# A two-layer hybrid decoder step: router products with the router's weights stationary, in three column groups of TensorE

## The reference, cut to what matters

```python
x = layer_norm(ALPHA * x + h, prm['ln_mix_g'][layer], prm['ln_mix_b'][layer])
f = moe_ffn(x, prm['w_router'], prm['b_router'], ...)

def moe_ffn(x, w_router, b_router, w_gate, w_up, w_down):
    xt = x.reshape(Bn * T, D)
    probs = jax.nn.softmax((xt @ w_router).astype(jnp.float32) + b_router, axis=-1)
    ...
```

## Time and profile before

| | us |
|---|---|
| runs (3) | 1962.90 to 1966.55, median 1966.42 |
| the profiled execution | 1965.85 |
| its span | 1963.7 |
| `mix_out`, first PE product to last logits | 964.8 to 1129.3 |
| `combine_pool_mix`, first POOL fill to last logits | 1430.5 to 1573.7 |

### The profile page before, as it was taken

One profiled execution on the slowest core, in us unless ns is written; L12 is line 12 of the kernel. 1 busy time (PEld: TensorE's weight loads), 2 busy tenths in 40 slices (PEclk: granted clock), 3 DMA queues, 4 the chain that ended last, 5 costly groups with the idle time before them and its releaser, 6 DMA issues. The chain is left out here.

```text
span 1963.7 us, 29748 instructions
## 1 busy us (share of the span) xinstructions
PE 1602.3 (82%) x11876; PEld 1020.5 (52%) x11877; DVE 709.9 (36%) x1129; ACT 347.3 (18%) x753; POOL 230.4 (12%) x275
## 2 busy tenths in 40 slices
PE   6999996765522999985399949999959949999978
PEld 5666564544212888873145434444439834444433
DVE  1000000744965555546533341111159641111117
ACT  1000001541311322322000001111112201111111
POOL 3000000003002222303000001001040001100121
PEclk7999997885555999997699959999959959999989
DMA  7224201100011000000411267877750268887634
GB/s 230 99 93 121 107 1 33 46 23 5 0 27 23 4 4 4 4 6 5 118 44 33 94 232 272 294 278 275 243 193 1 88 211 282 288 289 240 212 141 168
DMA packets 134252, 237.09 MB, mean 121 GB/s; under 512 B 20434, under 2 KB 94147, under 8 KB 133866
## 3 DMA queue, kind: packets, MB, share of 16 engines
q1 hardware_dynamic: 110642, 150.94, 23.6%
q0 software_dynamic: 16880, 60.46, 8.4%
q10 hardware_dynamic: 6624, 24.12, 3.0%
HBM read 178.82 MB, written 58.21 MB: 121 GB/s over the span
## 5 line engine op out<-in xcount | busy, mean ns | idle before, releaser
L1985 PE MATMUL ex_pb<-ew_w_gate_up,ex_xT 128*128 x736 | 330.1, 602 | 5.9 <-DVE ex_xT L2025 2.3
L222 PE MATMUL pj_pb<-pj_xT,pj_w 128*128 128x344 f32 (+3 forms) x960 | 282.1, 457 | 0.4 <-ACT pj_xT L232 0.4
L222 PEld LDWEIGHTS pj_pb<-pj_xT,pj_w 128*128 128x128 f32 (+1 forms) x960 | 180.8, 188 | 101.2 <-issue 1.7
L1985 PEld LDWEIGHTS ex_pb<-ew_w_gate_up,ex_xT 128*128 128x128 f32 x736 | 137.9, 192 | 165.3 <-issue 164.4
L1968 PE MATMUL ex_pb<-ew_w_down,ex_hiddenT 128*128 x368 | 165.7, 593 | 3.4 <-ACT ex_hiddenT L2050 3.4
L2174 DVE TENSOR_TENSOR ex_hidden<-ex_hidden,ex_pb 128x256 f32<-128x256 f32 x46 | 19.4, 421 | 324.6 <-ACT ex_hidden L2045 324.6
L1968 PEld LDWEIGHTS ex_pb<-ew_w_down,ex_hiddenT 128*128 128x128 f32 x368 | 66.3, 190 | 69.9 <-issue 69.9
L1932 POOL COPY ex_tokens_now<-ex_token_of_slot 128x1 uint32 (+1 forms) x48 | 9.5, 199 | 745.5 <-PE ex_pb L1957 399.7
L1741 PE MATMUL mo_pb<-mo_w,projected 128*128 128x512 f32 (+1 forms) x144 | 65.8, 611 | 21.3 <-DMA mo_w<-in_w_out 21.3
L2169 DVE COPY ex_y_rows<-ex_pb 128x512 f32<-128x512 f32 x46 | 31.8, 692 | 134.5 <-PE ex_pb L1968 134.5
L238 DVE COPY projected<-pj_pb 128x344 f32<-128x344 f32 (+3 forms) x21 | 10.9, 519 | 187.9 <-PE pj_pb L222 187.9
(11 more groups left out here) (422 smaller groups left out, 2429.5 us busy)
## 6 DMA issues: line engine op xcount, KB each, us to landing
ew_w_gate_up<-in_w_ex_gate SPq DMA_DIRECT2D x32, 1024.0 KB
ew_w_gate_up<-in_w_ex_up SPq DMA_DIRECT2D x32, 1024.0 KB
ew_w_down<-in_w_ex_down SPq DMA_DIRECT2D x32, 1024.0 KB
scratch_slots_out<-ex_y_rows ACTq DMA_DIRECT2D x46, 512.0 KB
scratch_slots_out<-pj_zero POOLq DMA_DIRECT2D x4, 4096.0 KB
scratch_x_stored<-x_rows SPq DMA_DIRECT2D x16, 512.0 KB
pj_w<-in_w_in SPq DMA_DIRECT2D x3, 2048.0 KB, 18.6
pj_xt<-in_x_prompt SPq DMA_DIRECT2D x8, 512.0 KB
```

What stands on the lines that cost most here:

```text
L222: last = nc.tensor.matmul(pb[0:mrows, 4 + at % 4, 0:tn], w[:, s % NW, k, c0:c0 + mrows], xT[:, k, t0:t0 + tn], start=(k == 0), stop=(k == ...
L1985: last = mm(pb[:, 2 + u, :], xT[:, u, k, :], w[:, k, :], start=(k == 0), stop=(k == KD - 1))
```

## The change

The router's product is turned round. The weights become the stationary side: a k-slice of `wr`, now 32 columns wide (the 16 columns twice), is loaded into column group g = k % 3 of TensorE, and xT streams past it with up to 128 token columns. The three groups write partitions 0 to 31, 32 to 63 and 64 to 95 of bank 6, each the sum of its own k-steps, with tokens along the free side. ScalarE copies these 96 x 128 partial sums to SBUF (`copy_parts`), and one more product (`router_sum`) with the parts as the stationary side and a 96 x 16 matrix `sel` of zeros and ones adds the three groups and turns the result, into bank 7. `take_logits` reads bank 7.

So that this fits in, router_sum(j) stands at the head of the TensorE iteration behind router(j), ahead of the next transposes; it waits for ev >= j (bank 7 emptied of tile j-1) and for copy_parts(j). VectorE takes the logits one iteration later than before, in both stages. copy_parts(j) stands behind norm_root in ScalarE's order, in the pooling stage ahead of first_gate. GpSimd makes `sel` with two small additions at the start of each stage (`group_sums`), in the pooling stage ahead of the gathers, and `w_router` is loaded twice.

```diff
+RG, RW = 3, 32
+def router_columns(pe, bank, wr, xT, n):
+    for k in range(KD):
+        g = k % RG
+        last = pe.matmul(bank[RW * g:RW * g + RW, 0:n], wr[:, k, :], xT[:, k, 0:n], start=(k < RG), stop=(k + RG >= KD))
+    return last
+def group_sums(pool, eng, sel, ident, sem):
+    eng.tensor_tensor(sel[:, :], ident[0:RG * RW, 0:E], ident[0:RG * RW, RW:RW + E], ALU.add).then_inc(sem, 1)
+    pool.wait_ge(sem, 1)
+    eng.tensor_tensor(sel[:, :], sel[:, :], ident[0:RG * RW, 2 * RW:2 * RW + E], ALU.add).then_inc(sem, 1)
@@ combine_pool_mix, GpSimd @@
             nc.gpsimd.tensor_scalar(alpha_i[:, :], const["ident"][:, :], ALPHA, None, ALU.mult).then_inc(q["alpha"], 1)
+            group_sums(pool, nc.gpsimd, sel, const["ident"], q["sel"])
             for j in range(TILES):
                 gather(j)
@@ combine_pool_mix, TensorE @@
             for s in steps:
+                if live(s - 4):
+                    router_sum(s - 4)
                 if live(s - 3):
                     transposes(s - 3)
@@ combine_pool_mix, ScalarE @@
                     norm_root(nc, act, qa, s + 1, rows(ORDER[s + 1]), sta, eps)
+                if live(s - 3):
+                    copy_parts(s - 3)
                 if live(s + 2):
                     first_gate(s + 2)
@@ combine_pool_mix, VectorE @@
-                if live(s - 4):
-                    take_logits(s - 4)
+                if live(s - 5):
+                    take_logits(s - 5)
@@ mix_out, TensorE @@
+            def router_sum(i):
+                n = rows(i)
+                if i == 0:
+                    pe.wait_ge(q["sel"], 2)
+                else:
                     pe.wait_ge(q["ev"], i)
+                pe.wait_ge(q["rpc"], i + 1)
+                nc.tensor.matmul(pb[0:n, 7, 0:E], part[:, 0:n], sel[:, :], start=True, stop=True).then_inc(q["rl"], 1)
-            for i in range(TILES + LAG):
-                if i >= LAG:
+            for i in range(TILES + LAG + 1):
+                if i > LAG:
+                    router_sum(i - LAG - 1)
+                if LAG <= i < TILES + LAG:
                     transpose_x(i - LAG)
                 if i < TILES:
                     products(i)
-                if i >= LAG:
+                if LAG <= i < TILES + LAG:
                     router(i - LAG)
@@ mix_out, ScalarE @@
+            def copy_parts(i):
+                n = rows(i)
+                act.wait_ge(q["rp"], i + 1)
+                if i:
+                    act.wait_ge(q["rl"], i)
+                nc.scalar.copy(part[:, 0:n], pb[0:RG * RW, 6, 0:n]).then_inc(q["rpc"], 1)
             for i in range(TILES + LAG):
                 if i >= LAG:
                     copy_x(i - LAG)
                 if i < TILES:
                     norm_root(nc, act, q, i, rows(i), st, eps)
+                if i >= LAG:
+                    copy_parts(i - LAG)
@@ mix_out, VectorE @@
             for i in range(TILES):
-                if i > LAG:
-                    take_logits(i - LAG - 1)
+                if i > LAG + 1:
+                    take_logits(i - LAG - 2)
...
-            for i in range(TILES - LAG - 1, TILES):
+            for i in range(TILES - LAG - 2, TILES):
                 take_logits(i)
```

More of the change, by code:

```diff
@@ L1445, in combine_pool_mix @@
         alpha_i = m.sb("alpha_ident", [P, P])
+        part = m.sb("logit_parts", [RG * RW, P])
+        sel = m.sb("group_sums", [RG * RW, E])
         pb = m.psum("pb", [P, 8, 512])
@@ L1449, in combine_pool_mix @@
         qb = {k: m.sem(f"b_{k}") for k in LN}
-        q = {k: m.sem(k) for k in "eps alpha first both wscaled band feats tr cp rl ev zero keep".split()}
+        q = {k: m.sem(k) for k in "eps alpha sel first both wscaled band feats tr cp rp rpc rl ev zero keep".split()}
         s_r = [m.sem(f"rows{i}") for i in range(TILES)]
         block = m.block()
-        steps = range(-1, TILES + 4)
+        steps = range(-1, TILES + 5)
         def x_(j):
@@ L1539, in router, with router_sum @@
             def router(j):
-                n = rows(ORDER[j])
                 pe.wait_ge(q["cp"], j + 1)
                 if j:
+                    pe.wait_ge(q["rpc"], j)
+                router_columns(nc.tensor, pb[:, 6, :], pm.wr, xT, rows(ORDER[j])).then_inc(q["rp"], 1)
+            def router_sum(j):
+                n = rows(ORDER[j])
+                if j == 0:
+                    pe.wait_ge(q["sel"], 2)
+                else:
                     pe.wait_ge(q["ev"], j)
-                for k in range(KD):
-                    last = mm(pb[0:n, 6, 0:E], xT[:, k, 0:n], pm.wr[:, k, :], start=(k == 0), stop=(k == KD - 1))
-                last.then_inc(q["rl"], 1)
+                pe.wait_ge(q["rpc"], j + 1)
+                mm(pb[0:n, 7, 0:E], part[:, 0:n], sel[:, :], start=True, stop=True).then_inc(q["rl"], 1)
             for s in steps:
+                if live(s - 4):
+                    router_sum(s - 4)
                 if live(s - 3):
@@ L1583, in copy_feats, with copy_parts @@
                     .then_inc(q["feats"], 1)
+            def copy_parts(j):
+                n = rows(ORDER[j])
+                act.wait_ge(q["rp"], j + 1)
+                if j:
+                    act.wait_ge(q["rl"], j)
+                nc.scalar.copy(part[:, 0:n], pb[0:RG * RW, 6, 0:n]).then_inc(q["rpc"], 1)
             first_gate(0)
@@ L1686, in mix_out @@
         w = m.sb("w", [P, KD, D])
-        wr = m.sb("w_router", [P, KD, E])
+        wr = m.sb("w_router", [P, KD, RW])
+        part = m.sb("logit_parts", [RG * RW, P])
+        sel = m.sb("group_sums", [RG * RW, E])
         g = m.sb("ln_g", [P, D])
@@ L1694, in mix_out @@
         pb = m.psum("pb", [P, 8, 512])
-        q = {k: m.sem(k) for k in "in w w_rwkv0 w_rwkv1 mm res st var root rs g x tr cp rl ev eps zero".split()}
+        q = {k: m.sem(k) for k in "in w w_rwkv0 w_rwkv1 mm res st var root rs g x tr cp sel rp rpc rl ev eps zero".split()}
         s_x = [m.sem(f"x{i}") for i in range(2)]
@@ L1727, in _ @@
             pool.dma_start(b[:, :], io["ln_mix_b"][0:1, :].to_broadcast([P, D])).then_inc(q["in"], 16)
-            pool.dma_start(wr[:, :, :], io["w_router"].rearrange("(k p) e -> p k e", p=P)).then_inc(q["in"], 16)
+            for e0 in range(0, RW, E):
+                pool.dma_start(wr[:, :, e0:e0 + E], io["w_router"].rearrange("(k p) e -> p k e", p=P)).then_inc(q["in"], 16)
+            group_sums(pool, nc.gpsimd, sel, const["ident"], q["sel"])
             nc.gpsimd.memset(lg[:, NT, :], 0.0).then_inc(q["zero"], 1)
```

28 lines of the change are left out of this document (16 added, 12 removed).

## The result

The change makes the kernel slower. Its median is 2008.24 us (4 runs, 2003.16 to 2010.13) beside 1966.28 us for the kernel before in the same session: a ratio of 1.021, 95% interval 1.0193 to 1.0228. The profiled execution took 2010.13 us with a span of 2007.9, which is 44.3 us more than the profiled execution of before; 44.1 of them lie in `mix_out`.

What follows compares the result with a forecast made beforehand. TensorE bounds `mix_out` (busy 16.35 of 16.35 us); in pooling VectorE is almost level. `mix_out` +40.5, second w_router load +0.3, pooling -3.75: +37 on 1965.85, median 2003; own range 1996 to 2010, with two rivals 1988 to 2014.

Steps and rivals of the forecast that it cites:

- Part 1, the products: Router product in both stages: 0.81 us (0.66 plus 0.15) instead of 1.71, then copy 0.27 and sum about 0.25.
- columns don't overlap: Rival: column groups run one after another, a router product takes 1.9 us instead of 0.8; +10 us, 2013; chance 0.08.
- Part 2, the waits: In `mix_out` router_sum waits for copy_parts in iteration 3 (2.2 us), for take_logits in iterations 4 to 8 (4.5 each).
- P: End of tile i's projection on TensorE in a `mix_out` iteration; transposes were to move from P + 1.55 to P + 6.1.
- Part 3, the clock: Half clock behind the `mix_out` waits: 2.3 us in five iterations (11.5), 1.0 in iteration 3; the profile row gave 2.5.
- clock holds: Rival: the clock stays full through the `mix_out` waits; 12.5 us and 1.5 of the end fall away, 1989; chance 0.11.
- Part 4, the end of `mix_out`: Last residual to last logits in `mix_out` grows from 11.3 to 14.6 us: +3.3 (bounds 1.5 and 5).
- Part 5, the pooling stage: Pooling stage: three steady steps -0.9 us, end -3.7, start +0.85 from additions ahead of the gathers; sum -3.75.
- faster: the saving counts: Rival: router_sum's waits don't count, each of 18 products gives 0.65 us; -12 us, 1954; chance 0.03.
- the waits to be half as long: Rival: `mix_out` waits are shorter, say only ScalarE's 2.2 us eight times, half clock after some; 1985; chance 0.06.

## Why the prediction was right

Forecast +37 us on the profiled execution and a median of 2003; measured +44.3 and 2008.2. Sign, mechanism and stage were right, and the time was inside the range. Point by point:

- **Part 1, the products.** 0.78 us each from first start to the start of what follows (1048.07 to 1048.85 in the kernel with the sum behind the projection; predicted 0.66 + 0.15 = 0.81), or 0.85 to the last end; the copy of the parts 0.24 to 0.26 (0.27). The rival "columns don't overlap" is excluded by these rows and by the kernel with one group (1.93). The rule that the prediction weighed, the Trainium skill's "TensorE: Matmul & The Clock Gate", Part 3, by which matmuls start and end in strict program order, would have given nine slots of 0.11 here, 0.98 us. The trace does not agree: in that product the passes start in six bunches (four of three and two of two) 0.11 to 0.13 us apart, with no more than 0.013 us between the starts of one bunch. Two passes of one group start 0.11 us apart (the kernel with one group), so the starts of a bunch belong to different groups, and a pass starts before the second pass of the product ahead of it.
- **Part 2, the waits.** As predicted, once ended by ScalarE (2.66 us) and then six times by VectorE's logits (4.9 to 5.0, the last one in the stage's end), and the transposes at P + 6.1, the predicted value. Wait per iteration 4.4 to 4.6 (predicted 4.5), and 2.1 (2.2) in iteration 3.
- **Part 3, the clock.** The mis-sized term. Half clock came behind every one of these waits, as expected, but cost 2.8 to 3.0 us instead of 2.3, and 1.7 instead of 1.0 in iteration 3 (3.8 us lost there, less the 2.1 of the wait). I had taken a price below my own row (2.5) on the ground that part of the low time would fall into the idle stretch; the stretches above show little of it there (mean clock 0.90 over the idle 4.7 us). Five iterations cost 37.1 us instead of 34.0, and iteration 3 cost 3.8 instead of 3.2. The rival "clock holds" (1989) came close in size to what the filled wait measured, 1986.15.
- **Part 4, the end of `mix_out`.** +2.8 (predicted +3.3), and the start +0.4 (0.3).
- **Part 5, the pooling stage.** -3.5 in all (predicted -3.75), a closeness that is in part luck: its pieces missed in both directions, and the same code gave -2.4 to -7.5 us in the other profiled executions (the -7.5 where the clock was back sooner). To the second logits +0.25 (with the first gather 0.46 later behind the first fill, predicted 0.85), three steady steps -1.1 (-0.9), the end -2.6 (-3.7).
- **Not predicted: the part behind the pooling stage, +3.1.** No line of it was touched, and I had put it at nothing. Of the 3.1 us, 2.9 lie in the very last TensorE products of the kernel, which run at half clock in the changed kernel and at full clock in the kernel before (rows in the last section). Why the clock falls sooner there is not explained.
- **The rival "faster: the saving counts"** named its deciding point: the place of the sum, one projection later. The run with just that gave 1959.2, where 1954 was put. For the waits to be half as long, the logits had to be off VectorE; that run gave 1980, where 1985 was put.

Together: 0.6 + 3.1 - 0.5 + 0.1 in `mix_out`, 0.3 in the experts, 0.3 in the pooling stage, 3.1 behind it and 0.2 ahead of `mix_out` make the 7.2 us between +37 and +44.

The Trainium skill's "TensorEngine Tiling (Array Packing)", Performance Considerations, recommends this swap of sides with column tiling for a narrow streaming side. The runs bear it out for the products (TensorE's time for one falls from 1.71 us to 0.78), and show what it leaves to the reader: a copy and a sum that need a place in an in-order queue.

## What to carry to other kernels

When a product is split into a fast part and a small dependent one, put the dependent one behind the largest piece of work in the same queue that doesn't need it. At the head of TensorE's queue this sum cost 44 us in its stage; behind one projection nothing waits for it, and the same instructions made the kernel 0.4% faster than before (0.9% with both stages set right). Before placing it, read from the timeline when each engine that it waits for reaches its step, counted from the end of the work just ahead: here P + 3.4 and P + 5.6, while the place offered P + 1.

## What the runs showed of the hardware

- Three column groups of 32, fp32: 16 passes of 128 columns in 0.85 us, and 1.93 us in a single group. Passes of different groups run side by side although the two passes of one product are neighbours in program order: sixteen passes start in six bunches.
- Idle TensorE and the clock, all in the steady part of `mix_out` and ahead of the same work: idle of 4.9 us, half clock behind each of five; 2.67 us, half clock behind five of six; 0.45 us, none. Filling most of the 4.9 us with unread products gave back 3.0 us an iteration.
- Code that nobody touched moves by some us. The part behind the pooling stage, the same code in all of these kernels, took 387.7 to 393.2 us in one profiled execution each (390.0 before, 393.1 after, 388.7 and 388.1 in the kernels with the sum moved, 392.4 with only the pooling stage changed). Its last TensorE products, in the timeline of the kernel after and then of before:

```profile
1994.75 1.91 PE L2295 MATMUL cb_pb<-x_rows,cb_alpha_ident 8*8 8x512 f32 x2
1996.45 3.62 PE L2297 MATMUL cb_pb<-cb_expert_rows,cb_gate_diagonals 8*8 8x512 f32 x4
```

```profile
1953.15 1.02 PE L2236 MATMUL cb_pb<-x_rows,cb_alpha_ident 8*8 8x512 f32 x2
1954.01 1.88 PE L2238 MATMUL cb_pb<-cb_expert_rows,cb_gate_diagonals 8*8 8x512 f32 x4
```

  In the kernel after, the clock falls to half 14 us before the end, while these products run, and TensorE had not been idle ahead of them; in the kernel before it falls some 8 us before the end, behind them. `mix_out` begins between 959.8 and 965.0 us in the ten profiled executions, with the same code ahead of it. And the pooling stage of the changed kernel took 135.7 to 140.8 us in the six kernels that share its code. So a difference of a few us between two kernels of this family can lie in a place that neither touched, and even the length of an edited stage tells what the edit did only piece by piece, where the clock is the same on both sides.
